# The first modulation group computed in eight output chunks, and the first weight slot's products placed between position-bias units

## Chip, cores, metric

The kernel runs on one core of a Trainium2 chip. The metric is the device time of one execution in microseconds (us). PE is the TensorE matmul engine, ACT ScalarE, DVE VectorE, POOL GpSimd, SP the SyncE queue that issues most DMAs.

## What is computed

Two blocks of a transformer on 512 tokens of width 1024, followed by further layers; the change lies in the first microseconds of block 0, which compute these lines:

```python
mod = jax.nn.silu(c) @ w_ada[l] + b_ada[l]
sh1, sc1, g1, sh2, sc2, g2 = jnp.split(mod[:, None, :], 6, axis=-1)
h = x * (1.0 + sc1) + sh1
...
proj = h @ w_in
...
bias = rel_bias[t5_bucket(q_pos[:, :, None] - k_pos)]
logits = (jnp.einsum('bqhd,bqkhd->bqkh', q, k_sel).astype(jnp.float32) * a_scale
          + bias.astype(jnp.float32))
logits = jnp.where(valid[..., None], logits, -jnp.inf)
```

## The kernel before

**Data.** Tokens lie along the free axis: x and h are eight chunks of 128 features by 512 tokens. Each weight and each h is split in a high and a low part (`w_hi`, `w_lo`, `h_hi`, `h_lo`), and a product is three matmuls, high x high, high x low, low x high. Weights come in slots of 128 x 2048 (1 MB), two buffers in turn: SP loads `w_raw`, ACT makes `w_hi` (`split_hi`, L1486), POOL makes `w_lo` (`lo`, L622) in four pieces of 512 columns. PE may begin a slot when its whole `w_lo` is there (`w_ready`). I call the first four slots of block 0 slot 0, W1, W2 and W3; each gives two tiles of 128 x 512, over eight chunks of h. Behind W3 stand index products (L1066), and then the pattern goes on in the same way for the whole kernel.

**First stage, up to slot 0.** Two things are made side by side.

The position bias: 32 units G, four query rows each for eight heads. For a unit DVE writes three rows of step functions (`steps`, L1974) and ACT one (`sign`, L1508), PE multiplies them by the bias differences (`bias_unit`, L819, 12 matmuls of 32 output rows), ACT adds a constant and writes `stage` (`out`, L1515), and SP stores it to the scratch `bias_scratch`. Columns are the keys: 128 for G below 8, 256, 384 and 512 for the others. ACT's order is sign of G + 3, then output of G; step buffers are four, PSUM banks four.

The modulation columns (shift and scale of the first norm, 16 columns of 128): eight ada slots of 1 MB, all issued by POOL at the start. A pair of slots gives 512 outputs of `silu(c) @ w_ada` as a row (`ada_slot`, L832), ACT copies the row out of PSUM, and `ada_columns` (L843) turns it into columns. After the fourth pair DVE adds the bias (`ada_take`, L2020), behind step rows 29. Then ACT makes `h_hi` chunk by chunk (`make_h`, L1504), DVE makes `h_lo` (`first_lo`, L2059), and PE runs `first_slot` (L1011): for every chunk four products with the high part and, one chunk behind, two with the low part. DVE's ten operations on rope angles (`angles`, L2047) stand behind its last `h_lo`.

All engines run their instructions in the order written; semaphores alone tie them together. Behind the units ACT's order is: `iq` copies of tiles 0 and 1, split of W2, two sine rows for rope, copies of tiles 2 and 3, split of W3.

## Time and profile before

| | us |
|---|---|
| median of 3 runs | 2330.14 |
| lowest, highest | 2330.11, 2334.72 |
| the profiled execution | 2329.42 |
| span of its profile | 2327.6 |
| PE busy in the span | 2288.7 (98%) |
| DVE, ACT, POOL busy | 1266.2, 1002.3, 997.7 |

The span is what the profiler saw from the first to the last instruction; the execution's own time is 1.8 us more. All clocks in the text count from the span's start. A row of a timeline gives start, duration, engine, line, operation, tiles and count; rows of one form that follow each other are merged. Durations overlap where an engine is pipelined, so start-to-start distances count.

### The profile page before, as it was taken

The page shows a single profiled execution, that of the slowest core. Times are in us where ns is not written, and L with a number is a line of the kernel's source. Part 1 is how long each engine was busy: PE and PEld are TensorE (multiplying, and loading weights), DVE is VectorE, ACT ScalarE, POOL GpSimd, SP SyncE. Part 2 cuts the span into 40 slices and gives each one's busy share as a digit, 9 for nine tenths or more (in the row PEclk, how much of TensorE's full clock was granted, in tenths as well). Part 3 has the DMA queues.
Part 4 walks back from the last instruction along what each step waited for, and adds up shares of the span by engine and source line. Part 5 has one row for each costly group of instructions (what it writes and reads, how often), then busy time and mean ns, then how long its engine had stood idle before and what let it go on. Part 6 is the DMA issues. An engine that isn't in the chain of part 4 may idle for free.

```text
span 2327.6 us, 32046 instructions
## 1 busy us (share of the span) xinstructions
PE 2288.7 (98%) x11302; PEld 1852.1 (80%) x11302; DVE 1266.2 (54%) x2679; ACT 1002.3 (43%) x1673; POOL 997.7 (43%) x894
## 2 busy tenths in 40 slices
PE   7999999999999999999999999999999999999998
PEld 4888878888888888887888888888888877788767
DVE  8765766844444378567486344315530163286684
ACT  7455455344342254544534443423142354333473
POOL 3432223544444453323245444445554434455472
PEclk9999999999999999999999999999999999999999
DMA  9641244332226354313442322223222321222210
GB/s 349 250 138 55 73 127 145 109 109 90 94 85 241 104 197 149 100 41 105 145 163 75 106 90 93 84 100 121 91 92 89 109 77 37 90 91 91 91 46 37
DMA packets 52645, 260.60 MB, mean 112 GB/s; under 512 B 6640, under 2 KB 16368, under 8 KB 26928
## 3 DMA queue, kind: packets, MB, share of 16 engines
q1 hardware_dynamic: 51376, 250.68, 31.2%
q0 software_dynamic: 1152, 8.39, 0.9%
q8 instruction: 70, 1.15, 0.2%
q14 instruction: 47, 0.39, 0.1%
HBM read 249.47 MB, written 7.34 MB: 110 GB/s over the span
## 4 chain that ended last, share of the span: by engine, by line
PE 70%; issue 16%; POOL 9%; DVE 3%; ACT 2%; DMA 1%; POOLq 0%; SPq 0%; DVEq 0%; ACTq 0%
PE bank L764 19%; PE bank L766 19%; PE bank L765 19%; POOL w_lo L618 8%; PE bank L1023 2%; PE bank L931 1%; PE bank L1283 1%; PE bank L1028 1%; PE bank L920 1%; PE bank L906 1%; DMA ada_early<-w_ada 1%; PE bank L1272 1%; PE bank L1437 1%; PE bank L881 0%; PE bank L1456 0%
## 5 line engine op out<-in xcount | busy, mean ns | idle before, releaser
L618 POOL TENSOR_TENSOR w_lo<-w_raw,w_hi 128x512 fp32r<-128x512 f32 (+2 forms) x732 | 878.9, 1233 | 1151.7 <-ACT w_hi L1489 766.9
L764 PE MATMUL bank<-h_hi,w_hi 128*128 128x512 f32 x1616 | 644.2, 399 | 0.8 <-POOL w_lo L618 0.7
L766 PE MATMUL bank<-h_hi,w_lo 128*128 128x512 f32 x1616 | 630.5, 390 | 0.0
L765 PE MATMUL bank<-h_lo,w_hi 128*128 128x512 f32 x1616 | 629.4, 389 | 0.0
L766 PEld LDWEIGHTS bank<-h_hi,w_lo 128*128 128x128 f32 x1616 | 303.3, 188 | 64.5
L764 PEld LDWEIGHTS bank<-h_hi,w_hi 128*128 128x128 f32 x1616 | 304.0, 188 | 61.9 <-issue 2.7
L765 PEld LDWEIGHTS bank<-h_lo,w_hi 128*128 128x128 f32 x1616 | 304.0, 188 | 59.0 <-issue 1.0
L1489 ACT ACTIVATE w_hi<-w_raw 128x2048 fp32r<-128x2048 f32 (+2 forms) x108 | 189.9, 1759 | 275.7 <-PE bank L766 254.8
L2411 DVE SCALAR_TENSOR_TENSOR cv<-bank,par,cv 128x511 f32<-128x511 f32 (+1 forms) x176 | 131.7, 749 | 211.9 <-ACT cv L1757 199.0
L1494 ACT ACTIVATE w_hi<-w_raw 128x2048 fp32r<-128x2048 f32 x68 | 129.9, 1910 | 125.3 <-PE bank L766 117.0
L1757 ACT ACTIVATE cv<-bank,par 128x512 f32<-128x512 f32 x88 | 68.4, 779 | 232.1 <-PE bank L766 230.8
L764 PE MATMUL bank<-u_hi,w_hi 128*128 128x512 f32 (+1 forms) x374 | 142.0, 380 | 0.8 <-POOL w_lo L618 0.8
L765 PE MATMUL bank<-u_lo,w_hi 128*128 128x512 f32 (+1 forms) x374 | 140.9, 377 | 0.0
L766 PE MATMUL bank<-u_hi,w_lo 128*128 128x512 f32 (+1 forms) x374 | 140.9, 377 | 0.0
L1555 ACT ACTIVATE L<-L,nmax 128x128 f32<-128x128 f32 (+3 forms) x128 | 72.0, 563 | 88.0 <-DVE nmax L2085 87.5
L764 PE MATMUL bank<-w_hi,h_hi 128*128 128x512 f32 x256 | 100.6, 393 | 0.0
L766 PE MATMUL bank<-w_hi,h_lo 128*128 128x512 f32 x256 | 99.8, 390 | 0.0
L765 PE MATMUL bank<-w_lo,h_hi 128*128 128x512 f32 x256 | 99.7, 389 | 0.0
L2460 DVE TENSOR_TENSOR rt<-bank,rope 32x512 f32<-32x512 f32 (+1 forms) x96 | 66.0, 688 | 33.6 <-PE bank L766 27.1
L2182 DVE SCALAR_TENSOR_TENSOR x<-bank,mod,x 128x512 f32<-128x512 f32 x28 | 21.0, 750 | 115.5 <-PE bank L766 111.0
L764 PEld LDWEIGHTS bank<-u_hi,w_hi 128*128 128x128 f32 x374 | 70.4, 188 | 14.9 <-POOL w_lo L618 1.6
L765 PEld LDWEIGHTS bank<-u_lo,w_hi 128*128 128x128 f32 x374 | 70.4, 188 | 13.3 <-issue 0.5
(386 smaller groups left out, 3827.2 us busy)
## 6 DMA issues: line engine op xcount, KB each, us to landing
w_raw<-w_stream SPq DMA_DIRECT2D x150, 1024.0 KB, 4.9
w_raw<-w_down SPq DMA_DIRECT2D x32, 704.0 KB, 4.1
ada_mid<-w_ada SPq DMA_DIRECT2D x20, 1024.0 KB, 5.1
...
```

Source lines behind the costliest of these rows:

```text
L618: ins = nc.gpsimd.tensor_tensor(w_lo[r][:, part], w_raw[r][:, part], w_hi[r][:, part].bitcast(fp32), ALU.subtract)
L764: nc.tensor.matmul(out, w[0][:, cols], xh, start=first, stop=False)
L765: nc.tensor.matmul(out, w[0][:, cols], xl, start=False, stop=False)
L766: return nc.tensor.matmul(out, w[1][:, cols], xh, start=False, stop=last)
L906: nc.tensor.matmul(banks[4 + t % 2][:, 0:n], q[0:96, h, i * P:(i + 1) * P], kk[0:96, h, 0:n], start=True, stop=True).then_inc(s_done, 1)
L1023: nc.tensor.matmul(banks[q][:, :], w[part][:, cols], xh[:, k, :], start=(k == 0 and part == 0), stop=False)
L1489: A_(w_hi[n % 2][:, 0:cols], w_raw[n % 2][:, 0:cols], ACT.Copy).then_inc(w_hi_done, 1)
L1494: A_(w_hi[n % 2][:, :], w_raw[n % 2][:, :], ACT.Copy).then_inc(w_hi_done, 1)
L1555: A_(L[t % 3][:, 0:n], L[t % 3][:, 0:n], ACT.Exp, bias=nmax[:, t:t + 1], scale=-1.0, accum_out=esum[:, t:t + 1]).then_inc(exp_done, 1)
L1757: A_(cv[s][c][:, :], banks[(t + c) % 4][:, :], ACT.Identity, bias=b, scale=w2).then_inc(conv_first, 1)
L2411: return V.scalar_tensor_tensor(out, banks[(t + c) % 4][:, 0:S - 2 + w], weight, out, ALU.mult, ALU.add)
L2460: V.tensor_tensor(rt2[q % 2][r ^ half:(r ^ half) + half, :], banks[q][r:r + half, :], rope[r:r + half, S:2 * S], ALU.mult).then_inc(rot, h ...
```

## The change

What moves, in words, with the new names:

- `seen(G)`: a unit now has 16 (G + 1) columns, from 16 to 512, which are the keys that its last query can see. The remaining columns up to the block's end are stored from the constant causal mask, 28 more stores (`TAILS`), issued by SP in the first attention between weight loads.
- The host lays the first eight ada slots out by output chunk: slot j holds the shift and scale columns of chunk j alone, so that one slot gives one chunk of mod. `ada_slot(j)` is eight matmuls of 256 columns instead of four of 512; `ada_columns(j)` is two instead of four for half as many columns.
- DVE adds and scales chunk by chunk behind the step rows of unit `MOD_AFTER[j]`; ACT makes `h_hi` of the chunk behind that unit's output; PE's products of chunk k (`first_chunk`, `first_chunk_low`) stand between the units from 19 to 28. Units 29 to 31 stand inside the first tile of W1.
- `w_hi` of slot 0 is made in quarters behind outputs 9 to 12, `w_lo` of slots 0 and 1 in 16 pieces of 128 columns. Ada slots 6 and 7 go to the buffers of 2 and 3 and are issued by POOL behind `w_lo` of slot 0. x and the first parameters are loaded near the start; W1's split stands behind output 26. The angles move behind DVE's two index low parts. PSUM banks of the units are three instead of four.

```diff
-        BIAS_BANKS = (2, 3, 6, 7)
-        ADA_AFTER = (8, 9, 11, 13, 16, 18, 21, 24)
+        BIAS_BANKS = (6, 7, 3)
...
+        def seen(G):
+            return 16 * (G + 1)
+        SLOT_AFTER = (8, 13, 18, 20, 22, 23, 24, 25)
+        COLS_AFTER = (9, 18, 19, 21, 23, 24, 25, 26)
+        MOD_AFTER = (18, 19, 20, 21, 23, 24, 25, 27)
...
+            sp.dma_start(par[0][:, :], a["par"][0]).then_inc(x_loaded, 16)
             weights(0, 0, a["w_stream"][0, 0])
+            sp.dma_start(x[:, :, :], a["x"]).then_inc(x_loaded, 16)
...
+            sp.wait_ge(ada_first[4], 16)
+            weights(0, 1, a["w_stream"][0, 1])
             sp.wait_ge(ada_first[7], 16)
-            weights(0, 1, a["w_stream"][0, 1])
+            weights(0, 2, a["w_stream"][0, 2])
...
-                if G == 28:
-                    weights(0, 2, a["w_stream"][0, 2])
...
+                    if l == 0 and SLOT_QK + 2 < m < SLOT_QK + 7:
+                        for i, G in TAILS[7 * (m - SLOT_QK - 3):7 * (m - SLOT_QK - 2)]:
+                            n, end = seen(G), (i + 1) * P
+                            sp.dma_start(bias_dram[4 * G:4 * G + 4, :, :, n:end].rearrange("a h q n -> (a h q) n"),
+                                         causal[:, 0:end - n]).then_inc(bias_stored[i], 16)
...
-            for k in range(8):
+            for k in range(6):
                 pool.dma_start(ada_early[k][:, :], a["w_ada"][k]).then_inc(ada_first[k], 16)
-            lo(slot_no(0, 0))
-            lo(slot_no(0, 1))
+            lo(slot_no(0, 0), SLOT, P)
+            for k in range(6, 8):
+                pool.wait_ge(ada_row, k - 3)
+                pool.dma_start(ada_early[k][:, :], a["w_ada"][k]).then_inc(ada_first[k], 16)
+            lo(slot_no(0, 1), SLOT, P)
...
+            def ada_slot(j):
+                pe.wait_ge(ada_first[j], 16)
+                if j:
+                    pe.wait_ge(ada_copied, j)
+                for k in range(KD):
+                    ins = nc.tensor.matmul(banks[4][32 * (k % 4):32 * (k % 4) + 32, 0:256], c_wide[:, k, :],
+                                           ada_early[j][:, 256 * k:256 * k + 256], start=(k < 4), stop=(k >= 4))
+                ins.then_inc(ada_row, 1)
+
+            def ada_columns(j):
+                pe.wait_ge(ada_copied, j + 1)
+                if j:
+                    pe.wait_ge(first_h, 2 * j - 1)
+                for part in range(2):
+                    at = 2 * j + part
+                    ins = nc.tensor.matmul(banks[5][:, at:at + 1], ada_rows[j % 2][:, part * P:part * P + P],
                                            selc[:, 9:10], start=True, stop=True)
-                return ins
-
-            for i, G in BIAS_UNITS:
+                ins.then_inc(ada_sum, 1)
...
+            def first_chunk(k):
+                w = split(0, SLOT_IDX)
+                if k == 0:
...
+                pe.wait_ge(h_hid, k + 1)
+                for q in range(2):
+                    for part in range(2):
+                        nc.tensor.matmul(banks[q][:, :], w[part][:, q * D + k * P:q * D + (k + 1) * P], h_hi[:, k, :],
+                                         start=(k == 0 and part == 0), stop=False)
+
+            def first_chunk_low(k):
+                w = split(0, SLOT_IDX)
+                pe.wait_ge(h_ready, k + 1)
+                for q in range(2):
+                    ins = nc.tensor.matmul(banks[q][:, :], w[0][:, q * D + k * P:q * D + (k + 1) * P], h_lo[:, k, :],
+                                           start=False, stop=(k == KD - 1))
+                    if k == KD - 1:
+                        ins.then_inc(tile_done, 1)
+
+            for i, G in BIAS_UNITS[:MOD_AFTER[KD - 1] + 2]:
                 bias_unit(i, G)
...
-            pe.wait_ge(par_loaded, 16 * 4)
+                if G in COLS_AFTER:
+                    ada_columns(COLS_AFTER.index(G))
+                if G in SLOT_AFTER:
+                    ada_slot(SLOT_AFTER.index(G))
+                if G - 1 in MOD_AFTER:
+                    k = MOD_AFTER.index(G - 1)
+                    first_chunk(k)
+                    if k:
+                        first_chunk_low(k - 1)
...
-                first_slot(l, SLOT_IDX, TILE_IDX, h_hi, h_lo, h_hid, KD * hidx(l, 0), h_ready, KD * hidx(l, 0))
-                for m in range(1, 4):
-                    if l == 0 and m == 1:
-                        pe.wait_ge(bias_out, 8 * NB)
+                if l:
+                    first_slot(l, SLOT_IDX, TILE_IDX, h_hi, h_lo, h_hid, KD * hidx(l, 0), h_ready, KD * hidx(l, 0))
+                else:
+                    first_chunk_low(KD - 1)
+                    wait_slot(0, SLOT_IDX + 1)
+                    for k in range(KD):
+                        ins = mm3(banks[2][:, :], split(0, SLOT_IDX + 1), slice(k * P, (k + 1) * P), h_hi[:, k, :],
+                                  h_lo[:, k, :], k == 0, k == KD - 1)
+                        if k in (1, 3, 5):
+                            bias_unit(*BIAS_UNITS[29 + k // 2])
+                    ins.then_inc(tile_done, 1)
+                    pe.wait_ge(bias_out, 8 * NB)
+                    tile(banks[3][:, :], split(0, SLOT_IDX + 1), D, h_hi, h_lo, KD).then_inc(tile_done, 1)
+                for m in range(1 if l else 2, 4):
...
+                if G in SLOT_AFTER:
+                    j = SLOT_AFTER.index(G)
+                    act.wait_ge(ada_row, j + 1)
+                    if j >= 2:
+                        act.wait_ge(ada_sum, j - 1)
+                    A_(ada_rows[j % 2][:, :], banks[4][:, 0:256], ACT.Copy).then_inc(ada_copied, 1)
+                if G in (9, 10, 11, 12):
+                    part = slice(512 * (G - 9), 512 * (G - 9) + 512)
+                    act.wait_ge(w_full[0], 16)
+                    ins = A_(w_hi[0][:, part], w_raw[0][:, part], ACT.Copy)
+                    if G == 12:
+                        ins.then_inc(w_hi_done, 1)
+                if G in MOD_AFTER:
+                    j = MOD_AFTER.index(G)
+                    act.wait_ge(x_loaded, 32)
+                    act.wait_ge(first_h, 2 * j + 1)
+                    make_h(j)
+                if G == 26:
+                    split_hi(0, 1)
...
-                if l == 0:
-                    for j in range(2, KD):
-                        make_h(j)
-                        if j == 3:
-                            split_hi(0, 1)
...
+            def first_mod(j):
+                if j == 0:
+                    dve.wait_ge(x_loaded, 32)
+                    chain(V.tensor_scalar(par[0][:, 8:16], par[0][:, 8:16], 1.0, None, ALU.add))
+                dve.wait_ge(ada_sum, j + 1)
+                V.tensor_tensor(mod[0][:, j:16:8], banks[5][:, 2 * j:2 * j + 2], par[0][:, j:16:8], ALU.add
+                                ).then_inc(first_h, 1)
+                dve.wait_ge(first_h, 2 * j + 1)
+                V.tensor_scalar(banks[2][:, :], x[:, j, :], mod[0][:, 8 + j:9 + j], mod[0][:, j:j + 1], ALU.mult,
+                                ALU.add).then_inc(first_h, 1)
+
+            def first_lo(j):
+                dve.wait_ge(first_h, 2 * j + 2)
+                dve.wait_ge(h_hid, j + 1)
+                V.tensor_tensor(h_lo[:, j, :], banks[2][:, :], f32(h_hi[:, j, :]), ALU.subtract).then_inc(h_ready, 1)
+
             for i, G in BIAS_UNITS:
                 steps(G)
-                if G == 29:
-                    dve.wait_ge(par_loaded, 16 * 4)
-                    ada_take(0, 0)
-            dve.wait_ge(x_loaded, 16)
+                if G - 1 in MOD_AFTER:
+                    first_lo(MOD_AFTER.index(G - 1))
+                if G in MOD_AFTER:
+                    first_mod(MOD_AFTER.index(G))
...
-            dve.wait_ge(ada_mod, 1)
-            for j in range(KD):
-                first_lo(j)
-            angles()
...
+                if l == 0:
+                    angles()
...
+        if l == 0:
+            ada[0] = np.concatenate([
+                np.asarray(w_ada[0])[:, 0:2048].reshape(KD, P, 2, KD, P).transpose(3, 1, 0, 2, 4).reshape(KD, P, SLOT),
+                ada[0][8:]])
```

Where it moves instructions, as the programs have them. First **PE, around the last ada slot before** (names with numbers are buffers; the tile's shape is output rows by columns), in the kernel before:

```order
L838 MATMUL bank5<-ada_early7_148,c_wide_174 32x512 x4
L828 MATMUL bank3<-step1_162,wb0_165 32x512 x4
L828 MATMUL bank3<-step1_162,wb1_166 32x512 x4
L828 MATMUL bank3<-step1_162,wb2_167 32x512 x4
L828 MATMUL bank6<-step2_163,wb0_165 32x512 x4
L828 MATMUL bank6<-step2_163,wb1_166 32x512 x4
L828 MATMUL bank6<-step2_163,wb2_167 32x512 x4
L828 MATMUL bank7<-step3_164,wb0_165 32x512 x4
```

and in the kernel after, from the ada slot of chunk 3 on:

```order
L852 MATMUL bank4<-ada_early3_144,c_wide_172 32x256 x8
L874 MATMUL bank0<-h_hi_56,w_hi0_52 128x512
L874 MATMUL bank0<-h_hi_56,w_lo0_54 128x512
L874 MATMUL bank1<-h_hi_56,w_hi0_52 128x512
L874 MATMUL bank1<-h_hi_56,w_lo0_54 128x512
L881 MATMUL bank0<-h_lo_57,w_hi0_52 128x512
L881 MATMUL bank1<-h_lo_57,w_hi0_52 128x512
L843 MATMUL bank6<-step1_160,wb0_163 32x352 x4
L843 MATMUL bank6<-step1_160,wb1_164 32x352 x4
L843 MATMUL bank6<-step1_160,wb2_165 32x352 x4
L862 MATMUL bank5<-selc_171,ada_rows1_150 128x1 x2
```

Before, ada slots and units alternate and the products of `h_hi` follow behind the last of 32 units; now a chunk's six products follow an ada slot and the next unit comes behind them.

**ACT, last outputs to the split of W2**, before:

```order
L1518 ACTIVATE stage36_214<-bank6,relc_172 128x512
L1518 ACTIVATE stage37_215<-bank7,relc_172 128x512
L1505 ACTIVATE h_hi_56<-x_49,mod0_63 128x512 x2
L1489 ACTIVATE w_hi1_53<-w_raw1_51 128x2048
L1505 ACTIVATE h_hi_56<-x_49,mod0_63 128x512 x4
L1647 ACTIVATE iq0_79<-bank0 64x512
L1647 ACTIVATE iq1_80<-bank0 64x512
L1647 ACTIVATE iq2_81<-bank1 64x512
L1647 ACTIVATE iq3_82<-bank1 64x512
L1489 ACTIVATE w_hi0_52<-w_raw0_50 128x2048
L1663 ACTIVATE rope_59<-ang3_183 128x512
```

and after, at output 26 (`stage32` is unit 26):

```order
L1561 ACTIVATE step1_160<-posf_173,qhalf_175 128x480
L1567 ACTIVATE stage32_208<-bank3,relc_170 128x432
L1538 ACTIVATE w_hi1_53<-w_raw1_51 128x2048
L1561 ACTIVATE step2_161<-posf_173,qhalf_175 128x496
L1567 ACTIVATE stage33_209<-bank6,relc_170 128x448
L1554 ACTIVATE h_hi_56<-x_49,mod0_63 128x512
```

and at the last outputs (`stage35` is unit 29, `stage37` unit 31):

```order
L1567 ACTIVATE stage35_211<-bank3,relc_170 128x480
L1567 ACTIVATE stage36_212<-bank6,relc_170 128x496
L1567 ACTIVATE stage37_213<-bank7,relc_170 128x512
L1698 ACTIVATE iq0_79<-bank0 64x512
L1698 ACTIVATE iq1_80<-bank0 64x512
L1698 ACTIVATE iq2_81<-bank1 64x512
L1698 ACTIVATE iq3_82<-bank1 64x512
L1538 ACTIVATE w_hi0_52<-w_raw0_50 128x2048
L1714 ACTIVATE rope_59<-ang3_181 128x512
L1715 ACTIVATE rope_59<-ang2_180 128x512
```

The split of slot 1 stood among the `h_hi` chunks behind all outputs and stands now behind output 26. Between the last output and the split of W2 stand only the four `iq` copies, as before, but output 31 now belongs to a unit that PE makes inside W1.

**POOL, ada slots and first low parts**, before:

```order
L643 DMA ada_early4_145<-w_ada 128x2048
L643 DMA ada_early5_146<-w_ada 128x2048
L643 DMA ada_early6_147<-w_ada 128x2048
L643 DMA ada_early7_148<-w_ada 128x2048
L618 ISA
L618 TENSOR_TENSOR w_lo0_54<-w_raw0_50,w_hi0_52 128x512 x4
L618 TENSOR_TENSOR w_lo1_55<-w_raw1_51,w_hi1_53 128x512 x4
```

and after:

```order
L655 DMA ada_early4_145<-w_ada 128x2048
L655 DMA ada_early5_146<-w_ada 128x2048
L630 ISA
L630 TENSOR_TENSOR w_lo0_54<-w_raw0_50,w_hi0_52 128x128 x16
L659 DMA ada_early6_147<-w_ada 128x2048
L659 DMA ada_early7_148<-w_ada 128x2048
L630 TENSOR_TENSOR w_lo1_55<-w_raw1_51,w_hi1_53 128x128 x16
```

The issues of ada slots 6 and 7 stood ahead of the first low part and stand now behind it, and that is made of 16 pieces.

## Rows read from the trace of the kernel before

**Rows 1.** The page, part 4: who carries the chain that ended last
```profile
PE 70%; issue 16%; POOL 9%; DVE 3%; ACT 2%; DMA 1%; POOLq 0%; SPq 0%; DVEq 0%; ACTq 0%
```

**Rows 2.** Windows: length, then busy PE, PEld, DVE, ACT, POOL; clock; DMA share; GB/s
```profile
8.90:44.80 35.90, 30.68 (x480) 15.43 (x481) 30.80 (x97) 32.07 (x66) 8.31 (x5) 0.95 1.01 388
44.80:56.10 11.30, 11.30 (x52) 9.04 (x49) 11.02 (x17) 6.91 (x10) 5.06 (x4) 1.00 0.96 312
56.10:67.20 11.10, 11.10 (x50) 9.18 (x49) 10.56 (x18) 6.61 (x9) 5.18 (x4) 1.00 0.85 352
67.20:78.10 10.90, 10.90 (x50) 8.76 (x49) 10.35 (x15) 4.29 (x5) 5.05 (x4) 1.00 0.75 289
```

**Rows 3.** PE's timeline, 8 to 57 us: start, us, line, tiles, count
```profile
27.89 1.64 PE L828 MATMUL bank<-step,wb 128*32 128x384 bf16 x36
...
29.35 1.03 PE L838 MATMUL bank<-ada_early,c_wide 128*32 128x512 f32 x8
...
30.80 1.05 PE L846 MATMUL bank<-selc,ada_rows 128*128 128x1 f32 x8
...
34.23 0.83 PE L828 MATMUL bank<-step,wb 128*32 128x512 bf16 x12 [0.28 <-issue]
```

**Rows 4.** The chain in order of time, 0 to 130 us: start, us, what
```profile
47.36 0.91 PE bank L1023 x4
48.27 0.45 PE bank L1028 x2
```

**Rows 5.** ACT's timeline, 0 to 60 us
```profile
9.57 0.37 ACT L1518 ACTIVATE stage<-bank,relc 128x128 f32<-128x128 f32 x1 [2.51 <-PE bank L828]
...
10.16 0.37 ACT L1518 ACTIVATE stage<-bank,relc 128x128 f32<-128x128 f32 x1
...
26.49 0.59 ACT L1518 ACTIVATE stage<-bank,relc 128x384 f32<-128x384 f32 x1
...
27.46 0.60 ACT L1518 ACTIVATE stage<-bank,relc 128x384 f32<-128x384 f32 x1
...
56.06 2.45 ACT L1647 ACTIVATE iq<-bank 64x512 fp32r<-64x512 f32 x4 [4.39 <-PE bank L1028]
...
58.54 1.92 ACT L1489 ACTIVATE w_hi<-w_raw 128x2048 fp32r<-128x2048 f32 x1
```

**Rows 6.** DVE's timeline, 38 to 125 us
```profile
43.81 0.80 DVE L2062 TENSOR_SCALAR bank<-x,mod 128x512 f32<-128x512 f32 x1
...
55.38 0.48 DVE L2048 TENSOR_SCALAR ang<-posf,ck 128x512 f32<-128x512 f32 x1
...
93.10 0.48 DVE L2300 TENSOR_SCALAR sel<-bank,iw_tok 128x256 f32<-128x256 f32 x1 [10.65 <-ACT bank L1674]
```

**Rows 7.** POOL's timeline: one piece, four pieces, sixteen small pieces
```profile
33.61 4.33 POOL L618 TENSOR_TENSOR w_lo<-w_raw,w_hi 128x512 fp32r<-128x512 f32 x1 [24.41 <-ACT w_hi L1489]
...
48.93 5.06 POOL L618 TENSOR_TENSOR w_lo<-w_raw,w_hi 128x512 fp32r<-128x512 f32 x4 [7.30 <-ACT w_hi L1489]
...
2197.16 6.87 POOL L618 TENSOR_TENSOR w_lo<-w_raw,w_hi 128x128 fp32r<-128x128 f32 x16 [6.84 <-ACT w_hi L1489]
```

**Rows 8.** Windows, 33.6 to 36.8 us
```profile
33.60:36.80 3.20, 2.42 (x36) 0.81 (x36) 3.20 (x9) 3.20 (x7) 3.19 (x1) 1.00 0.99 387
```

**Rows 9.** Windows of PE alone: length, PE busy; granted clock; DMA share; GB/s
```profile
37.20:38.60 1.40, 0.03 (x4) 1.00 1.04 304
...
39.50:42.80 3.30, 2.84 (x26) 0.50 1.10 364
```

**Rows 10.** SP's timeline, 0 to 130 us
```profile
28.99 0.33 SPq L506 DMA_DIRECT2D x<-x  x1
31.44 0.33 SPq L489 DMA_DIRECT2D w_raw<-w_stream  x1
31.82 17.98 SPq L512 DMA_DIRECT2D bias_scratch<-stage  x29
```

**Rows 11.** PE's timeline, 88 to 91 us: the first index product
```profile
89.37 0.28 PE L1066 MATMUL bank<-ik_hi,iq 128*128 128x256 f32 x1
```

82 lines of the change are left out of this document (24 added, 58 removed).

## Prediction

> **What bounds the kernel now.** I read the page's chain first: PE carries 70% of it and "issue" between PE instructions another 16% [rows 1]. Then the windows by stage: before 44.8 us PE is busy for 30.7 of 35.9 us, and from 44.8 on it is busy all the time, through the first slot (to 56.1), W1 (to 67.2) and W2 (to 78.1) [rows 2]. So a microsecond by which the first stage ends earlier or later moves the whole run, as long as nothing behind it has to be waited for. That is the reader's question: when does PE end W1, W2 and W3, and does it still run without a gap? The mark that I follow is PE's first index product behind W3, at 89.37 us [rows 11].
>
> **What is there to gain.** Of the 35.9 us before 44.8, 5.2 us are idle on PE. The shorter rows (16 to 512 columns instead of 128 to 512) take the 32 units from 10,240 columns to 8,448. Three 384-column units took 1.64 us, a 512-column one 0.83 [rows 3]; at 0.2 us a unit plus 0.00125 us a column this is 2.2 us less. More than some 7 us can't be gained.
>
> **The change, step by step (my clock is the span of the profiled execution).**
>
> *Up to the first chunk.* ACT sets the pace here: after each unit it writes a sign row and an output, 0.59 us a pair at 128 columns (9.57 to 10.16) and 0.97 at 384 (26.49 to 27.46) [rows 5], so 0.39 + 0.0015 per column. It starts output 0 at about 9.5, as now (9.57), after four signs and 2.5 us of idling [rows 5]. From there to the end of the quarter splits behind unit 12 it has 12 signs and 13 outputs, 12.5 pairs of some 140 columns at 0.60 (7.5 us), a row copy (0.4) and a split of slot 0 in quarters, 2.0 where the whole is 1.92 [rows 5]: 9.5 + 9.9 = 19.4. Then POOL makes w_lo of slot 0, in 16 pieces: 6.87 us in the one place where such pieces stand [rows 7], so 26.4 at the earliest. But POOL does not get on while DVE makes step rows: the piece begun at 33.61 took 4.33 us against the 1.27 of a quarter of [rows 7]'s 5.06, and for 3.2 us beside it DVE ran nine rows without a gap [rows 8]. Between 19.4 and 28 DVE has step rows for about four more units; I put 1.7 us on it. First chunk at 28.2, while unit 19 and column sum 2 leave PE at about 25: 3 us idle.
>
> *First chunk to the end of slot 0.* PE's own work: eight chunks of 0.91 + 0.45 us [rows 4], 10.9 us; units 20 to 28 at 0.6, 5.4; slots 3 to 7 (a start-to-start of 0.87 within a 1.03 row) 4.3; column sums 3 to 7, half of 1.05 each, 2.5 [rows 3]. That is 23.1. On top of it come waits for DVE, since step rows of the next unit stand behind the chunk's x*scale+shift: the add into mod (my estimate for two columns 0.2), the product 0.80 [rows 6], three step rows at 0.36 (nine in 3.20 us, [rows 8]), 2.05 in all, against 1.37 us which PE has in hand after the column sum. That is 0.7 us for five units, and 0.6 at chunk 7, which waits for ACT's output 27 and h. 23.1 + 4.2 = 27.3: slot 0 ends at 55.5. Before it ended at 56.1, and three units are still owed.
>
> *W1 waits.* ACT's split of slot 1 stands behind output 26. PE ends unit 26 at 49.2 (two chunks, three lows, two units, a column sum and 1.4 of waits before 55.5); output and split (0.7 + 1.9) end at 51.8. POOL's 16 pieces then take 6.87 [rows 7], and the step rows of units 28 to 31, which DVE makes in this time, block them for another 3.5 to 4 (nine rows in 3.2 to 3.5 us [rows 8], and the tail of unit 28). W1 can start at 63.0, not at 56.1: **+6.8**, of which PE stands still for 7.4 us. In the kernel before, the same w_lo took 5.06 us from 48.93 [rows 7] and was there two microseconds before it was wanted. Units 29 to 31 inside W1 cost 3 x 0.7 = **+2.1**: W1 ends at 76.0, before at 67.2.
>
> *W2 waits too.* On ACT outputs 28 to 31, the four iq copies and the split of slot 2 stand in this order, and output 31 needs unit 31, which PE ends 6.2 us into W1: 69.2. Output with hand-over 0.8, copies 2.45 and split 1.9 [rows 5] give 74.2 to 74.4. POOL's four pieces take 5.06, and DVE's angles, which began at 55.38 with POOL idle [rows 6] and now begin at about 74, stand beside them: seven of the ten are of the step rows' kind, 0.48 us like the first [rows 6], which is 3 at most with hand-overs. W2 starts at 82.4; PE would have wanted it at 76.0: **+6.4**. Sum at W2: 6.8 + 2.1 + 6.4 = 15.3.
>
> *After that.* W3's split waits for the angles (81), the rope sines and two copies (84.8), then 1.9 and 5.1: 91.8, while W2 ends at 93.4. No further wait. DVE has 10.65 us of idle time before the first index product [rows 6], so that it can take the angles and both ada passes. The loads behind the bias stores come after output 31 (70): two ada slots and W3's weights land by 79. Cover is enough, and the mark moves by 15.4.
>
> *Loads of ada slots 6 and 7.* They are issued by POOL only after w_lo of slot 0, at 28. In the kernel before SP went on behind slot 6 at 28.99 and behind slot 7 at 31.44 [rows 10]: 2.45 us for 1 MB. Up to slot 5 the same bytes must land (x instead of slots 6 and 7), so 31; then W1's weights, 6 and 7: 38. PE wants slot 7 at 45. Seven microseconds in hand, priced at nothing; if the cover went, each microsecond of delay would count once.
>
> *The 28 stores of constant tails* stand in SP's queue in the first attention, seven ahead of each of four weight loads. A store took 0.62 us of SP (29 in 17.98, [rows 10]), so 4.3 a load; a buffer is free for loading a slot early, and a slot is 11 us of PE [rows 2]. Nothing, or 1 us.
>
> **The clock.** After 1.4 us in which PE did nothing at 37.2 the granted clock was 0.5 (1.2 GHz) from 39.5 to 42.8 [rows 9], 3.3 us in which it did the work of 1.65. The new order has three longer gaps (3, 7.4 and 6.4 us). One such stretch behind each costs 1.65; the first is half covered by waits for DVE. That is **+4** (0 to +9).
>
> The Trainium skill (TensorE: Matmul & The Clock Gate, "What's actually happening") says that the throttled state is the default and activity releases it. This case's rows agree as far as [rows 9] go. By that rule the lightly loaded PE of the stage could stay at 1.2 GHz between chunks as well; that is rival D below.
>
> **Sum.** 15.4 + 4 = 19.4 us. The profiled execution took 2329.42 us, 0.7 under the median of 2330.14, so 2330.1 + 19.4: **2349.5 us**.
>
> **Rivals.**
> A, the forecast: both waits stand, POOL is held off by step rows and angles. 2344 to 2356. Chance 0.60.
> B, POOL is not held off in this way (the 4.33 us was a single case; small pieces may slip between rows). W1 then starts at 58.5 and W2 at 75.0, the mark moves by 7.8, and with 3 for the clock it is 2337 to 2343. For it: the pieces are four times smaller; against it: DVE's nine rows had no gap at all in [rows 8]. Chance 0.18.
> C, not slower: chunks hide better than I think. It decides at the start of W1. Without a hold the first chunk starts at 26.4, 23.1 us of PE work bring the end of slot 0 to 49.6, w_lo of slot 1 is ready at 54.3, 1.8 earlier than W1's start before. Then W1 ends at 67.4, but output 31, copies, split and w_lo still put W2 at 70.6 against 67.2: +3.4, 2333.5, which counts as no change. To be faster the chain behind output 31 would have to be shorter than its rows. Chances 0.07 for this, 0.03 for faster, down to 2325.
> D, worse: the clock stays at 0.5 for longer stretches, or ada slots 6 and 7 come after 45. PE's 23.1 us at half speed for a third of the time are 8 more; 2356 to 2368. For it: the drop at 39.5 came after a gap of only 1.4 us [rows 9]. Against it: in the same stage PE was never busier than between chunks now. Chance 0.12.
> That the change doesn't do what it says: chunks would stand in the code between units and yet run bunched behind w_lo of slot 0. That is partly so in A (unit 20 on waits for chunk 0), and it gives A's time.
>
> **How the numbers follow.** Likeliest 2349.5. The range takes in B and A, and leaves out C, faster, and the upper half of D, 0.16: 2337 to 2360. A measurement of this kernel tells 0.2% (4.7 us) from no change. Faster 0.03, same 0.07, slower 0.90.
>
> **What would show it.** PE's first L874 at 28 (26 to 31). Slot 0's last product at 55.5 (50 in C). A gap on PE of 5 to 8 us ahead of the first product of W1 that names POOL's w_lo, and one of 4 to 7 ahead of W2. POOL's 16 pieces for slot 1 over 9 to 11 us instead of 6.9 (6.9 in B). The first index product at 105 to 110 instead of 89.4, and the rest of the trace shifted by the same amount. Clock rows at 0.5 behind these gaps. I am wrong if PE has no gap ahead of W1 or W2, or if the index products stand before 94.

## The result, and the profile after

The changed kernel takes **2349.6 us** (median of 4 runs, 2348.6 to 2351.0), the kernel before 2330.1 beside it: a ratio of 1.008, with a 95% interval of 1.0068 to 1.0092. The forecast was 2349.5. The profiled execution took 2348.61 us with a span of 2346.8, against 2329.42 and 2327.6 before: 19.2 us more. So the total was met almost exactly. Several of its terms were not, and the experiments and the last table say which.

PE's timeline of the changed kernel (start, us, then line, tiles and count; in brackets the idle time before the row and what ended it) has the places that the prediction named. L874 are a chunk's products, L779 to L781 those of a whole slot, L843 a bias unit, L852 an ada slot, L862 column sums, L1115 the index products.

```profile
17.05 1.94 PE L852 MATMUL bank<-ada_early,c_wide 128*32 128x256 f32 x16 [3.15 <-DMA ada_early<-w_ada]
...
31.63 0.58 PE L862 MATMUL bank<-selc,ada_rows 128*128 128x1 f32 x4 [1.97 <-DVE mod L2089]
32.07 0.48 PE L874 MATMUL bank<-h_hi,w_hi 128*128 128x512 f32 x1
...
46.15 0.69 PE L843 MATMUL bank<-step,wb 128*32 128x400 bf16 x12 [1.20 <-DVE step L2031]
...
59.77 1.07 PE L881 MATMUL bank<-h_lo,w_hi 128*128 128x512 f32 x4
65.34 0.79 PE L779 MATMUL bank<-h_hi,w_hi 128*128 128x512 f32 x1 [4.50 <-POOL w_lo L630]
65.94 0.63 PE L780 MATMUL bank<-h_lo,w_hi 128*128 128x512 f32 x1
...
84.85 0.50 PE L779 MATMUL bank<-h_hi,w_hi 128*128 128x512 f32 x1 [4.14 <-POOL w_lo L630]
...
109.26 0.28 PE L1115 MATMUL bank<-ik_hi,iq 128*128 128x256 f32 x1
```

The first chunk starts at 32.1, slot 0 ends at 60.8 (before 56.1 [rows 2]), and the two forecast gaps are there, 4.50 us ahead of W1 and 4.14 ahead of W2, both naming POOL's w_lo. The mark (PE's first index product) stands at 109.26, 19.9 behind [rows 11]; from there on the two traces stay between 19.2 and 20.3 us apart. What was not forecast is the first row: PE waits 3.15 us for ada slot 0. ACT's timeline shows what that delays: the row copy, for which ACT waits 4.72 us, and with it the quarter splits of slot 0, of which the last ends at 24.5 where the prediction had 19.4.

```profile
19.06 0.38 ACT L1581 ACTIVATE ada_rows<-bank 128x256 f32<-128x256 f32 x1 [4.72 <-PE bank L852]
...
23.87 0.63 ACT L1585 ACTIVATE w_hi<-w_raw 128x512 fp32r<-128x512 f32 x1
```

POOL's timeline shows the same from the other side. The pieces of slot 0 took 7.22 us, those of slot 1 8.34, those of slot 2 6.04; the rows by which the prediction priced them took 6.87, 6.87 and 5.06 [rows 7].

```profile
24.59 7.22 POOL L630 TENSOR_TENSOR w_lo<-w_raw,w_hi 128x128 fp32r<-128x128 f32 x16 [16.19 <-ACT w_hi L1585]
...
56.95 8.34 POOL L630 TENSOR_TENSOR w_lo<-w_raw,w_hi 128x128 fp32r<-128x128 f32 x16 [21.15 <-ACT w_hi L1538]
78.76 6.04 POOL L630 TENSOR_TENSOR w_lo<-w_raw,w_hi 128x512 fp32r<-128x512 f32 x4 [13.47 <-ACT w_hi L1538]
```

Windows of the changed kernel (length, busy PE, PEld, DVE, ACT, POOL, granted clock, DMA share, GB/s): behind each of the two gaps the clock is low, which answers to [rows 9]; in these stretches products start 0.43 us apart instead of 0.23. Counted product by product, the one behind W1's gap costs 1.3 us and the one behind W2's 1.6.

```profile
65.60:68.80 3.20, 3.20 (x18) 1.79 (x18) 0.00 (x0) 0.00 (x0) 0.00 (x0) 0.60 0.00 0
69.00:72.00 3.00, 3.00 (x21) 1.87 (x22) 0.00 (x0) 1.29 (x2) 0.00 (x0) 1.00 0.23 87
86.10:89.30 3.20, 3.20 (x11) 2.49 (x10) 3.06 (x6) 2.03 (x4) 0.00 (x0) 0.60 0.00 0
```

### The profile page after: what moved, and what is told of

It reads as the page before. It is cut to its first block, busy times and chain, and to the rows that moved or that the text cites. A ratio compares the mean times of both kernels' runs of the same rounds, so it can differ in the third digit from the quotient of the medians.

```text
span 2346.8 us, 32266 instructions
## 1 busy us (share of the span) xinstructions
PE 2294.2 (98%) x11366; PEld 1856.8 (79%) x11366; DVE 1270.2 (54%) x2686; ACT 999.8 (43%) x1680; POOL 1000.4 (43%) x918
## 4 chain that ended last, share of the span: by engine, by line
PE 80%; issue 10%; POOL 4%; DVE 3%; ACT 2%; DMA 1%; SPq 0%; POOLq 0%; DVEq 0%; ACTq 0%
PE bank L779 22%; PE bank L781 22%; PE bank L780 22%; POOL w_lo L630 4%; PE bank L1062 2%; PE bank L970 1%; PE bank L1332 1%; PE bank L1067 1%; PE bank L959 1%; PE bank L945 1%; PE bank L1321 1%; DMA ada_early<-w_ada 1%; PE bank L1486 1%; PE bank L920 0%; PE bank L1505 0%
## 5 line engine op out<-in xcount | busy, mean ns | idle before, releaser
L779 PE MATMUL bank<-h_hi,w_hi 128*128 128x512 f32 x1616 | 645.8, 400 | 9.4 <-POOL w_lo L630 9.4
L781 PE MATMUL bank<-h_hi,w_lo 128*128 128x512 f32 x1616 | 631.7, 391 | 0.0
L779 PEld LDWEIGHTS bank<-h_hi,w_hi 128*128 128x128 f32 x1616 | 304.6, 189 | 72.2 <-POOL w_lo L630 10.4
L781 PEld LDWEIGHTS bank<-h_hi,w_lo 128*128 128x128 f32 x1616 | 303.9, 188 | 65.0
L779 PE MATMUL bank<-u_hi,w_hi 128*128 128x512 f32 (+1 forms) x374 | 141.7, 379 | 0.0
L781 PE MATMUL bank<-u_hi,w_lo 128*128 128x512 f32 (+1 forms) x374 | 140.9, 377 | 0.0
L779 PE MATMUL bank<-w_hi,h_hi 128*128 128x512 f32 x256 | 100.7, 393 | 0.0
L781 PE MATMUL bank<-w_hi,h_lo 128*128 128x512 f32 x256 | 99.7, 390 | 0.0
L779 PEld LDWEIGHTS bank<-u_hi,w_hi 128*128 128x128 f32 x374 | 70.4, 188 | 13.4 <-issue 0.5
```

Source lines behind the costliest of these rows:

```text
L779: nc.tensor.matmul(out, w[0][:, cols], xh, start=first, stop=False)
L781: return nc.tensor.matmul(out, w[1][:, cols], xh, start=False, stop=last)
```

## The experiments

All times are medians; the range and the ratio to the kernel before say how sure they are. A ratio is always to the kernel before as it was measured beside that run: 2330.2 for e1 to e4, 2330.7 for e5 to e8, 2331.4 for e9 to e12. "First chunk", "W1" and "mark" are the starts of the first product of slot 0, of W1's first product and of the first index product in the profiled execution. Executions of one kernel differ by 2 us and more through low-clock stretches that come and go, here and later in the run, so the marks tell more than the medians where these are 2 us apart.

| kernel | first chunk | W1 | mark | us (range, runs) | ratio, 95% |
|---|---|---|---|---|---|
| before | - | 56.1 | 89.37 | 2330.1 | 1 |
| after | 32.07 | 65.34 | 109.26 | 2349.6 (2348.6-2351.0, 4) | 1.0068-1.0092 |
| e1 units 29-31 ahead of W1 | 32.28 | 68.34 | 105.65 | 2342.0 (2340.7-2349.7, 4) | 1.0028-1.0062 |
| e2 split of slot 1 early | 32.15 | 63.51 | 106.05 | 2345.6 (2342.2-2346.3, 4) | 1.0041-1.0075 |
| e3 both | 31.61 | 64.94 | 102.32 | 2344.5 (2341.5-2347.7, 4) | 1.0043-1.0076 |
| e4 x behind ada slot 1 | 35.96 | 70.65 | 114.65 | 2354.2 (2353.8-2354.5, 4) | 1.0082-1.0116 |
| e5 x in two loads | 28.86 | 62.28 | 106.41 | 2347.3 (2345.5-2351.4, 4) | 1.0063-1.0094 |
| e6 = e3 + angles early | 32.24 | 65.50 | 98.83 | 2339.4 (2337.8-2340.5, 5) | 1.0023-1.0050 |
| e7 = e6 + x in two loads | 29.00 | 68.11 | 101.45 | 2340.5 (2337.4-2341.6, 5) | 1.0025-1.0052 |
| e9 = e7, split a little later | 28.90 | 61.44 | 94.82 | 2336.3 (2335.2-2336.7, 10) | 1.0009-1.0028 |
| e10 filler ahead of W1 | 32.08 | 69.83 | 112.46 | 2352.8 (2351.4-2354.2, 4) | 1.0076-1.0107 |
| e12 w_lo in four pieces | 36.05 | 68.97 | 112.52 | 2350.8 (2347.1-2353.1, 4) | 1.0061-1.0092 |
| e8 before, short rows only | - | - | 88.71 | 2330.6 (2327.1-2334.2, 11) | 0.9991-1.0009 |
| e11 = e8 + filler | - | - | 88.34 | 2330.2 (2328.0-2333.8, 11) | 0.9987-1.0005 |

### The two waits: e1, e2, e3

e1 moves three lines on PE:

```
                     first_chunk_low(KD - 1)
+                    for i, G in BIAS_UNITS[29:]:
+                        bias_unit(i, G)
                     wait_slot(0, SLOT_IDX + 1)
...
-                        if k in (1, 3, 5):
-                            bias_unit(*BIAS_UNITS[29 + k // 2])
```

> The changed kernel (2349.6 us) with bias units 29 to 31 put on PE ahead of W1 instead of inside it; nothing else. Theory: W2 waits because output 31, on ACT ahead of the iq copies and the split of slot 2, needs unit 31, which stands inside W1. With the units in the gap ahead of W1 (PE idle 4.50 us there, step rows ready by 64.6) W1 starts at 65.5 to 66.5, output 31 ends by 67.5, w_lo of slot 2 is ready at 76, and the gap of 4.14 us ahead of W2 goes, with the low-clock stretch behind it (1.7) and the 2.1 us of the units, less about 1 for a later start of W1: 2342.5 (2340.5 to 2344.5). Rival: W2's wait is POOL being held off by DVE's angles; then 2 us or more of that gap stay and the time is 2346 or more.

Measured: 2342.0, the gap ahead of W2 is gone. The profiled execution was the outlier at 2349.67: right behind the first chunk its clock was 0.54 from 33 to 39 us, where the changed kernel has 1.00, and further low stretches (819 to 829 and near 2259 us) took it from 16.3 us behind the kernel before at the mark to 20.3 at the end. The chain unit 31, output 31, copies, split, w_lo is shown; POOL being held is not what makes W2 wait. A new wait comes up ahead of W3:

```profile
92.71 0.41 PE L1091 MATMUL bank<-ck,iw_row 8*128 8x8 f32 x4 [1.89 <-DVE kr_raw L2334]
```

e2 takes the split out of its place behind output 26:

```
+                if G in (20, 21, 22, 23):
+                    q = (20, 21, 22, 23).index(G)
+                    part = slice(512 * q, 512 * q + 512)
+                    act.wait_ge(w_full[1], 16)
+                    ins = A_(w_hi[1][:, part], w_raw[1][:, part], ACT.Copy)
+                    if q == 3:
+                        ins.then_inc(w_hi_done, 1)
...
-                if G == 26:
-                    split_hi(0, 1)
```

> The changed kernel with ACT's split of slot 1 in quarters behind outputs 20 to 23 instead of whole behind output 26. Theory: W1 waits only because that split comes late; its w_lo is then ready by 55, W1 starts at the end of slot 0 (60.8, at most 1 us later), the 4.50 us gap ahead of W1 goes with its low-clock stretch (1.7); the gap ahead of W2 stays at about 4 us because output 31 still stands inside W1. 2343.9 (2342.5 to 2346). Rival: POOL's pieces and DVE's step rows get in each other's way wherever they meet, so the pieces now delay the step rows that the chunks wait behind; slot 0 then ends at 63 or later and the time is 2347 to 2350.

Measured: 2345.6, inside the theory's range. W1 follows slot 0 without a gap, W2 still waits 4.13 us. But slot 0 ends at 63.5, which is the rival's figure (63 or later) and not the theory's 60.8. The rival's reason did not bring it: PE's waits for step rows and h are 0.66, 1.20, 0.27 and 0.40 us, against 0.66, 1.20, 0.24 and 0.62 in the changed kernel. This trace, too, has the low clock behind the first chunk, and by unit 21 it is already 2.7 us behind the changed kernel.

> Both edits at once: units 29 to 31 ahead of W1, and the split of slot 1 in quarters behind outputs 20 to 23. Theory: neither W1 nor W2 waits for w_lo; 4.5 + 4.1 us of gaps and 3.4 us of lost clock go, but step rows 29 to 31 must now be done before W1, which may cost 1 to 2 us on PE: 2338.5 (2336.5 to 2341). What is left against the kernel before (2330.1) is then the late first chunk. Rival: one wait takes the other's place (step rows 29 to 31 ahead of W1), so that the two edits together bring no more than the better one: 2342 to 2344.

Measured: 2344.5, and by its time the rival seems right. But step rows cost only 0.33 and 0.38 us ahead of W1. What took the place of the two gaps is the one ahead of W3, as in e1. PE's timeline of e3:

```profile
64.94 0.50 PE L779 MATMUL bank<-h_hi,w_hi 128*128 128x512 f32 x1
...
89.31 0.41 PE L1091 MATMUL bank<-ck,iw_row 8*128 8x8 f32 x4 [1.89 <-DVE kr_raw L2339]
```

From W1 to the mark e3 takes 37.4 us where the kernel before takes 33.3 (56.1 to 89.37). DVE is late there: its angles now stand ahead of kr_raw, and its timeline shows that they meet POOL's pieces for slot 2 (70.09 to 76.20) as well.

```profile
70.16 1.50 DVE L2124 TENSOR_SCALAR ang<-ang 128x512 f32<-128x512 f32 x1
71.69 1.67 DVE L2125 SCALAR_TENSOR_TENSOR ang<-ang,ang 128x512 f32<-128x512 f32 x1
```

### The angles: e6

e6 is e3 with the call of the ten angle rows moved from behind the first two index_lo to a place right behind the last step rows, where POOL stands idle.

> The kernel with both edits (units 29 to 31 ahead of W1, split of slot 1 early; 2344.5 us, first index product at 102.3), and DVE's ten angle rows put right behind the step rows, as in the kernel before, instead of behind the first two index_lo. Theory: DVE's 9 us of angles in the middle of W1 and W2 make kr_raw late, for which PE waits 1.89 us ahead of W3, and the low clock of 3.4 us behind it costs 1.7 more; both go: first index product at 98.5 to 99.5, 2341 (2339.5 to 2343). POOL's four pieces for slot 2 then take 5.1 us instead of 6.1. Rival: DVE is late for another reason (its ada pass, or the order of its waits), PE still waits over 1 us ahead of W3, and the time stays at 2343.5 or more.

Measured: 2339.4, 0.1 under the theory's range; mark 98.83, W1 to mark 33.3 us as in the kernel before, no gap ahead of W3. The second of the rows above is L2125 here as well, and takes 0.69 us instead of 1.67; POOL's four pieces take 5.07 instead of 6.11. The ten angle rows take 5.4 us instead of 9.3, so that 3.9 us of DVE's delay was the meeting and the rest the place in the order; which of the two alone would have cleared the 1.89 us no run separates:

```profile
65.48 0.43 DVE L2124 TENSOR_SCALAR ang<-ang 128x512 f32<-128x512 f32 x1
65.94 0.69 DVE L2125 SCALAR_TENSOR_TENSOR ang<-ang,ang 128x512 f32<-128x512 f32 x1
```

### The loads: e4, e5, e7, e9

> The changed kernel with the load of x issued behind ada slot 1's landing instead of at the start; nothing else. Theory: the first chunk came 3.9 us later than forecast because x (2 MB, queued by SP at 4.04 us) shares the DMA engines with ada slot 0, for which PE waits 3.15 us at 17.05. With x later, ada slot 0 lands by 14.5, the whole stage moves 3 us forward, first chunk at 28.5 to 29.5, and the total goes down by 3 (2 to 4): 2346.6. Rival: the bytes up to x and ada slot 5 are the same, so what is won at slot 0 is lost again at x (wanted at 28) or at slots 4 and 5: first chunk at 31 or later, 2349 to 2351.

Measured: 2354.2, worse than the theory and than its rival's figure too, though of the rival's kind. PE no longer waits for ada slot 0, but DVE's first use of x does:

```profile
29.59 0.17 DVE L2088 TENSOR_SCALAR par<-par 128x8 f32<-128x8 f32 x1 [8.65 <-DMA x<-x]
```

PE then stands idle for 5.97 us ahead of its row at 30.10, and its clock is low afterwards (mean 0.52 from 30 to 40 us). That gap is not where the low clock began: it was 0.50 already from 23.0 to 24.2, ahead of the gap, after a stretch of small units with waits of 0.75, 0.76 and 0.52 us between them.

```profile
23.00:24.20 1.20, 1.13 (x17) 0.29 (x12) 0.00 (x0) 1.20 (x4) 1.20 (x4) 0.50 0.99 410
```

So x is in the way at the start and missing if it is put off whole; e5 splits it:

```
-            sp.dma_start(x[:, :, :], a["x"]).then_inc(x_loaded, 16)
+            sp.dma_start(x[:, 0:2, :], a["x"][:, 0:2, :]).then_inc(x_loaded, 16)
...
+            sp.wait_ge(ada_first[1], 16)
+            sp.dma_start(x[:, 2:KD, :], a["x"][:, 2:KD, :]).then_inc(par_loaded, 16)
```

> The changed kernel with x loaded in two parts: chunks 0 and 1 (512 KB) where the whole was queued, chunks 2 to 7 behind ada slot 1's landing. With x wholly behind slot 1 (the run before) slot 0 of ada no longer held up the stage, but x landed only at 29.6 and DVE waited 8.65 us for it. Theory: x's bytes ahead of ada slot 0 cost 3 to 4 us and nothing else does, so with a quarter of them the first chunk stands at 28.5 to 30 instead of 32.1, chunks 2 to 7 land before they are wanted (36), all behind moves along, and the first index product comes at 106 to 107 instead of 109.3: 2346.5 (2345 to 2348). Rival: the start of the first chunk is bound by ACT's outputs and DVE's step rows anyway: 31 or later, no change, 2349 to 2351.

Measured: 2347.3, as the theory said. PE's wait for ada slot 0 falls from 3.15 to 0.27 us, the first chunk comes at 28.86 (forecast for the changed kernel: 28.2), the mark at 106.41:

```profile
13.84 1.94 PE L854 MATMUL bank<-ada_early,c_wide 128*32 128x256 f32 x16 [0.27 <-DMA ada_early<-w_ada]
```

This shows the larger part of the first term's miss: 3.2 of the 3.9 us of start, and 2.9 of mark.

> All four edits at once: units 29 to 31 ahead of W1, split of slot 1 early, angles early, x in two loads. Theory: the gains add: first index product at 95.5 to 97, and no gap ahead of W1, W2 and W3; what is left against 89.4 of the kernel before is the stage itself, in which PE stands idle more (7.9 us of the 23 between 9 and 32 us in the changed kernel, 2.1 in the kernel before). 2337.5 (2335.5 to 2340), so slower than before even then. Rival: the late start was wholly the loads' doing, and with it gone the new order is level with the kernel before: first index product at 92 or earlier, 2333 or less.

Measured: 2340.5; the gains did not add. The split's first quarter stood on ACT behind output 20, and W1's weights, now behind the rest of x, were not there. ACT's timeline:

```profile
38.03 0.63 ACT L1594 ACTIVATE w_hi<-w_raw 128x512 fp32r<-128x512 f32 x1 [5.79 <-DMA w_raw<-w_stream]
```

A wait on an in-order engine holds everything behind it: PE then waited 4.93 us for h_hi, and its clock was 0.50 from 39 to 44 us. e9 puts the quarters behind outputs 22 to 25 and changes nothing else.

> The kernel with all four edits once more, with the quarters of the split of slot 1 behind outputs 22 to 25 instead of 20 to 23. In the run before, the first chunk stood at 29.0, but ACT then waited 5.79 us for W1's weights (landed at 38.0, since the second part of x is now ahead of them) with all its outputs behind. Theory: only that wait spoiled it; with the quarters behind output 22 (after 38) slot 0 ends 3 us earlier than in the kernel without the split load of x, and the first index product stands at 95.5 to 97 (98.8 there): 2336.5 (2335 to 2338.5), still slower than the kernel before (2330.7). Rival: w_lo of slot 1 now comes too late for W1 (quarters end near 48, pieces at 56), or DVE's waits eat it: 98 or later, 2339 or more.

Measured: 2336.3, mark 94.82, and the ten runs lie within 1.5 us; the profiled one has no low clock before the mark. What is left is the start of W1 alone, 61.4 against 56.1; from there to the mark the two take 33.4 and 33.3 us. Windows of e9, then the same three stages of the kernel before:

```profile
9.00:28.90 19.90, 15.29 (x300) 9.52 (x300) 16.24 (x62) 17.67 (x48) 7.49 (x17) 1.00 1.02 417
28.90:61.40 32.50, 28.16 (x294) 16.16 (x293) 25.63 (x58) 20.24 (x36) 8.95 (x18) 1.00 0.72 258
61.40:94.80 33.40, 33.40 (x152) 27.38 (x149) 24.65 (x37) 15.66 (x20) 16.39 (x13) 1.00 0.84 321
```

```profile
9.00:44.80 35.80, 30.68 (x480) 15.40 (x481) 30.70 (x97) 32.07 (x66) 8.21 (x5) 0.95 1.01 387
44.80:56.10 11.30, 11.30 (x52) 9.04 (x49) 11.02 (x17) 6.91 (x10) 5.06 (x4) 1.00 0.96 312
```

PE stands idle for 4.6 + 4.3 us where it was 5.1, and is busy for 43.5 where it was 42.0, although the rows are shorter and the 42.0 hold the half-clock stretch of [rows 9]. The products now come in eight small groups: from the first product of such a group to the next unit 1.59 us pass (31.62 to 33.21 in e9), where six products in a row took 0.91 + 0.45 [rows 4]. Not every wait is repaired, though. PE's longest one behind the first chunk is new:

```profile
55.95 0.77 PE L845 MATMUL bank<-step,wb 128*32 128x464 bf16 x12 [1.79 <-DVE step L2040]
```

In the changed kernel this wait was 0.24 us. Here POOL's pieces of slot 1 (50.16 to 58.30) meet the step rows of units 27 and 28, three of which take 1.77 and 1.71 us instead of 1.17 and 1.19. So about 1.5 of the 5.3 us belong to where e9 puts the split; my estimate for the new order itself is the remaining 3.8. No run had all these waits gone, and the best one of the new order, this one, is still 0.1 to 0.3% slower than the kernel before.

### The clock: e10

> The changed kernel with 34 idle matmuls (128x128 by 128 columns, 0.12 us each from one to the next where they stand elsewhere in this kernel) on PE between the last product of slot 0 and the wait for w_lo of slot 1, so that PE is busy for 4.1 us of the 4.50 us gap; they compute nothing that is used. Theory: the granted clock of 0.5 from 65.5 on follows from PE's gap; with the gap filled this stretch of 3.4 us does not come, W1's first products stand 0.23 us apart instead of 0.43, and all behind is 1.7 us earlier: first index product at 107.5, 2347.9 (2346.8 to 2349). The stretch behind the gap ahead of W2 stays. Rival: the low clock comes for another reason (a beat of its own, or the load of the whole stage); it then stands at the same place, and the time stays at 2349 to 2350.

The time missed both theories: 2352.8. Each filler matmul left two records in the trace, so 34 of them took 7.75 us, not the 4.1 that I had reckoned from the spacing of records; W1 started 2.9 us after w_lo was there (POOL ends at 66.95), and the time says nothing of the clock. The trace does. PE's timeline and windows of e10:

```profile
62.32 7.75 PE L817 MATMUL bank<-ck 128*128 128x128 f32 x68
69.83 0.47 PE L779 MATMUL bank<-h_hi,w_hi 128*128 128x512 f32 x1
70.14 0.39 PE L780 MATMUL bank<-h_lo,w_hi 128*128 128x512 f32 x1
```

```profile
65.60:68.80 3.20, 3.20 (x32) 3.20 (x31) 0.62 (x2) 0.00 (x0) 1.35 (x3) 1.00 0.00 0
69.00:72.00 3.00, 3.00 (x28) 2.08 (x26) 0.00 (x0) 0.00 (x0) 0.00 (x0) 1.00 0.00 0
```

Without the gap W1 starts at full clock, and the unfilled gap ahead of W2 (4.16 us) still has its low stretch. That the low clock at W1 follows from PE's gap is shown, and with it the price: from W1's first product to its last e10 takes 1.3 us less than the changed kernel. All nine gaps of 4.1 to 4.5 us ahead of W1 or W2 in these traces (the changed kernel, e2, e4, e5, e10, e12) are followed by such a stretch, and where W1 comes without one (e2, e3, e6, e7, e9) the clock there is full. Behind shorter gaps it is less regular: of the six profiled executions whose first chunk came at 31.6 to 32.3, all with a gap of 1.5 to 2.0 us ahead of it, five had low clock there (e1, e2, e3, e6, e10) and the changed kernel's own had not; the three with the first chunk at 28.9 to 29.0 and a gap of 1.97 had none. What decides there is open.

### POOL and DVE: e12

> The changed kernel with w_lo of slots 0 and 1 in four pieces of 512 columns each, as the kernel before makes them, instead of 16 of 128. Theory that the forecast went by: a POOL piece that meets DVE's step rows is held until they pause (4.33 us for a piece of 1.27), so large pieces do worse beside the dense step rows 29 to 31: slot 1's w_lo takes 8 us or more and W1 starts no earlier than now (65.3), while slot 0's pieces, which meet few rows, take 5.1 to 6.5 instead of 7.2. Rival: in both orders the two engines just share, and the piece size costs only its own time (5.06 against 6.87): then W1 starts 1.8 us earlier or more, at 63.5 or before, and the time is 2347.5 or less.

Both halves of my theory fell, and the rival's earlier W1 (63.5 or before) and shorter time did not come either: 68.97 and 2350.8. Slot 1's pieces took 5.43 us, not 8, although step rows 29 to 31 came 2.4 us behind their start as before; they were hardly held. It was DVE that was held: one step row took as long as a whole piece. DVE's and POOL's lines of e12, 25 to 29 us (count, then duration in ns: least, median, most):

```profile
L2031 DVE TENSOR_SCALAR step<-posf,qpos x3: 1039/1374/1384, 25.1 to 27.3; 128x304 bf16<-128x304 f32 x3
```

```profile
L630 POOL TENSOR_TENSOR w_lo<-w_raw,w_hi x4: 1272/1335/1341, 24.7 to 28.5; 128x512 fp32r<-128x512 f32 x4
```

The same two kinds of instruction in the changed kernel, with pieces of a quarter of the size, 59 to 65 us:

```profile
L2031 DVE TENSOR_SCALAR step<-posf,qpos x9: 462/667/673, 59.4 to 63.9; 128x480 bf16<-128x480 f32 x3, 128x496 bf16<-128x496 f32 x3, 128x512 bf16<-128x512 f32 x3
```

```profile
L630 POOL TENSOR_TENSOR w_lo<-w_raw,w_hi x16: 446/619/630, 57.0 to 64.8; 128x128 fp32r<-128x128 f32 x16
```

So the two take turns, and a row lasts about as long as the other engine's piece. Unit 18 started 1.88 us late that way (the row names ACT's output; its own three step rows ended at 28.71, just ahead of it), the clock fell for 13 us (0.52 from 29.3 to 42.7), and the first chunk came at 36.05. At W1 the larger pieces paid: its gap is 1.59 us instead of 4.50. In time the two kernels can't be told apart (2350.8, from 2347.1 to 2353.1, against 2349.6), so which size is better is open.

The Trainium skill (SBUF — State Buffer, "Who interferes with whom") describes a pair of ports that the two engines share, for DVE's `tensor_scalar` among others, as an exclusive lock, held for the whole instruction by whoever issues first, and says that issue order, not op shape, decides who blocks. The rows here agree that either engine can be the one that pays. They don't show strict turns of whole instructions: a row and a piece together took 0.667 us, less than the 0.79 that the two add up to alone (0.36 and 0.43). Nor do they say why nine DVE rows could keep POOL waiting in [rows 8] and again in e8. The kernel before shows both orders in one trace. Its first piece was held for DVE's nine rows; 3 us later, beside the fourth piece, it was a DVE row that took 1.57 us (its instructions on L1980, 40 to 44.5 us):

```profile
L1980 DVE TENSOR_SCALAR step<-posf,qpos x6: 474/475/1572, 40.3 to 43.4; 128x512 bf16<-128x512 f32 x6
```

### One part alone: e8, e11

> The kernel before with one part of the change alone: rows of 16 (G+1) columns for unit G in step rows, units, outputs and stores, and the constant tails stored in the first attention; ada slots, column sums, loads, splits and slot 0 as before. Theory: ACT's pair falls by 0.0015 us a column and DVE's rows likewise, PE's units by 2.2 us in all, and with 28 tails costing nothing the run is 2 us faster: 2328.2 (2326.5 to 2329.7), first index product at 87 to 88. Rival: 28 more stores in SP's queue hold up the weight loads of the first attention; 2331 to 2334, with the first index product early and the loss behind 200 us.

Measured: 2330.6, no change (0.9991 to 1.0009), and not by the rival's way either: the mark is only 0.7 us earlier. PE's waits for ada slots are still there (0.31, 0.96 and 0.42 us), and the clock was low for twice as long, from 38.4 to 45.0:

```profile
33.00:38.20 5.20, 3.23 (x47) 1.39 (x39) 2.78 (x8) 5.20 (x11) 5.15 (x3) 0.93 0.96 353
38.40:45.00 6.60, 6.60 (x56) 3.00 (x56) 5.33 (x11) 5.62 (x10) 2.20 (x2) 0.55 0.88 276
```

> The kernel before with short rows (2330.6 us, first index product at 88.7, granted clock 0.5 for 6.8 us from 38.2 on), and 8 idle matmuls on PE ahead of the last column sums, where it waited 1.24 us for ACT. Theory: the low clock there takes what the short rows save; without it the last four units take 3.3 us instead of 5.1 and the first index product stands at 86 to 87: 2328.5 (2327 to 2330), faster than both kernels. Rival: slot 0 is bound by w_lo of slot 0 or by h, not by the units, and starts at 44.5 as now; or the low clock comes all the same: 2330 to 2331.

Measured: 2330.2, the rival's time; the mark, at 88.34, is 1.3 us later than the theory's range. The low clock is gone, but DVE's rows met POOL's pieces of slot 0 in the other way round this time: nine rows took 7.52 us (up to 1.47 each) while POOL needed 5.59 instead of 7.56, and units 29 to 31 waited 0.34, 0.50 and 0.38 us for them. Slot 0 started at 43.78 instead of 44.49. So in these two runs what the rows save went to waits for loads, to the clock or to the turn-taking; how it divides between them is not shown. No version that I ran beats the kernel before by more than can be measured.

## Why the prediction was right, and where it was right by luck

| step | forecast, us | measured, us | its own length, forecast; measured |
|---|---|---|---|
| first chunk | 28.2 | 32.1 | |
| slot 0 ends | 55.5 | 60.8 | 27.3; 28.8 |
| W1 starts | 63.0 | 65.3 | gap 7.4; 4.5 |
| W1 ends | 76.0 | 80.7 | 13.0; 15.4 |
| W2 starts | 82.4 | 84.9 | gap 6.4; 4.1 |
| mark | 104.8 without the clock, 105 to 110 with it | 109.26 | |

- **The two waits held.** They stand where they were said to stand, and e2 and e1 take them away one by one. The mark moves by 19.9 us where 15.4 and some of the 4 for the clock were forecast. Rival C falls with the two gaps. D did not come in the changed kernel, where the clock was full from 29 to 42 us; e4 and e12 have its long low stretch.
- **Rival B does not fall.** It said that POOL is hardly held off. Its gaps come out at 3.0 us ahead of W1 (58.5 less 55.5) and 3.5 ahead of W2 (75.0 less 58.5 and the 13.0 of W1); the forecast's are 7.4 and 6.4, and 4.50 and 4.14 were measured. Its 2337 to 2343 with a start 5.3 us later would be 2342 to 2348 (my estimate), so the time alone does not tell the two apart by much. POOL's 16 pieces for slot 1 took 8.34 us, between B's 6.9 and the forecast's 9 to 11. Of the signs that the prediction named, the first product of slot 0 (26 to 31), its end, the gap ahead of W1 (5 to 8) and these pieces missed; the gap ahead of W2, the mark and the low clock behind the gaps came.
- **First chunk, +3.9.** The step that failed is "9.5 + 9.9 = 19.4" for the end of the quarter splits (measured 24.5). It reckoned ACT's work only, and had no term for the 4.72 us that ACT waits for ada slot 0. It took that slot's landing from the kernel before; the order of the loads that the diff shows (x queued at 4.04 us, ahead of everything but slot 0's weights) was read for slots 6 and 7 and not for slot 0. e5 shows 3.2 us of it. The next term erred the other way: DVE's rows were to hold the pieces of slot 0 by 1.7 us and did so by 0.35. The forecast for slots 6 and 7, nothing, was right.
- **POOL held off, 3.5 to 4 us at slot 1 and 3 at slot 2.** Measured 1.5 and 1.0. The term had the right partner and looked at one victim only: beside step rows and angles DVE paid as much as POOL did or more (nine rows in 5.2 us instead of 3.2 [rows 8]; four angle rows of 1.37 to 1.65 us instead of 0.43 to 0.69). In e12 DVE paid nearly all of it. The sum at W1 is also rounded up: 51.8 + 6.87 + 3.5 to 4 is 62.2 to 62.7, where the forecast has 63.0.
- **The shorter rows.** The price of 0.2 us a unit plus 0.00125 a column gives 0.68 us for 384 columns, while the row beside it has three such units in 1.64, 0.55 each. The 2.2 us saved by it are not in the sum; e8 shows 0.7 at the mark.
- **Slot 0, 1.5 us longer than forecast,** by two errors that partly cancel. PE's own work was put at 23.1 us and took 26.0: 1.59 us from a chunk's first product to the next unit instead of 1.36, and about 1.0 an ada slot instead of 0.87. Its waits were put at 4.2 us and took 2.9 (0.66, 1.20 and 0.24 for step rows, 0.62 for chunk 7, and small ones).
- **W1 and its units.** The 13.0 us of the forecast are 14.05 without the low clock (e10) and 15.4 with it: a unit inside W1 costs about 1.0 us and not 0.7.
- **Clock, +4.** Two stretches of the three came, at the two longer gaps, and cost 2.9 us. A third stood at 1257 us in this execution (granted clock 0.56 from 1256.8 to 1259.8), where the kernel before had none; it moved the two traces apart by only 0.4 us.
- **Luck.** Slot 0 ended 5.3 us late and the two gaps were 5.2 us shorter than forecast. Nothing ties these two: the gap ahead of W1 runs from a split that stands a fixed 4 us ahead of the end of slot 0. With the gaps as measured and the start as forecast, the sum would have been 2344.3; with the start as measured and the gaps as forecast, 2354.8.
- **The stage itself.** The sum had no term for what stays when both waits are gone. e9 puts it at 5.3 us at W1, of which about 1.5 come from its own split.
